# A decoder layer in split float32: the two output tiles of a weight unit take turns term by term

## The reference

```python
x = x + 0.5 * ((silu(h1 @ w1) * (h1 @ w3)) @ w2)        # h1 = rmsnorm(x), hidden width 5632
h = rmsnorm(x)                                          # model width 2048
z = h @ w_in                                            # 8 sections of 1024 columns
oa = block-sparse causal attention(z), or = retention(z), om = cross-attention(z)
gates = sigmoid(h @ w_gate + b_gate)                    # 3 x 2048 columns
merged = g_a * (oa @ w_br_moba) + g_r * (or @ w_br_ret) + g_m * (om @ w_br_mem)
x = x + merged @ w_out
x = x + 0.5 * SwiGLU_2(rmsnorm(x))                      # same shapes as the first line
y = rmsnorm(x)
```

## Time and profile before

| | |
|---|---|
| median of 3 runs | 2692.11 us (2691.68 to 2693.47) |
| span of the profiled execution, first to last instruction | 2688.8 us |
| median less span: what lies around the span | 3.3 us |
| PE busy | 2662.4 us, 99% |
| weight loads (PEld) busy, beside PE | 2590.7 us, 96% |
| DVE busy | 1541.8 us, 57% |
| ACT busy | 1092.0 us, 41% |
| mean rate of DMA | 223 GB/s |

### The profile page before, as it was taken

How to read it: one execution, slowest core, us unless ns; L and a number is a source line. 1 busy time by engine, 2 the same in 40 slices (tenths; PEclk the granted TensorE clock), 3 DMA queues, 4 the chain that set the end, 5 groups by cost and what they waited for, 6 DMA issues and landing times.

```text
span 2688.8 us, 50855 instructions
## 1 busy us (share of the span) xinstructions
PE 2662.4 (99%) x21748; PEld 2590.7 (96%) x21748; DVE 1541.8 (57%) x2442; ACT 1092.0 (41%) x985; POOL 147.5 (5%) x266
## 2 busy tenths in 40 slices
PE   8999999999999999999999999999999999999998
PEld 7899999999999999999998988999999999999998
DVE  4545554555547778876675744365554545555455
ACT  6433333333335433455352444344433333333345
POOL 0000000000000011211211121100000000000000
PEclk9999999999999999999999999999999999999999
DMA  7665555555555799799979899766555555555553
GB/s 267 235 210 186 176 185 182 177 187 177 185 168 175 237 306 299 240 354 392 339 274 334 280 317 320 232 211 198 173 188 175 185 184 177 185 176 186 181 159 115
DMA packets 487449, 600.08 MB, mean 223 GB/s; under 512 B 12608, under 2 KB 447008, under 8 KB 485984
## 3 DMA queue, kind: packets, MB, share of 16 engines
q1 hardware_dynamic: 442512, 456.37, 52.9%
q0 software_dynamic: 35088, 129.74, 13.3%
q10 hardware_dynamic: 9680, 11.54, 1.2%
HBM read 575.16 MB, written 24.53 MB: 223 GB/s over the span
## 4 chain that ended last, share of the span: by engine, by line
PE 96%; DVE 1%; DMA 1%; ACT 1%; issue 1%; DVEq 0%; POOLq 0%; SPq 0%; ACTq 0%
PE PS L554 30%; PE PS L555 29%; PE PS L556 29%; PE PS L1997 1%; PE PS L590 1%; PE PS L592 1%; PE PS L591 1%; DVE splitL L509 1%; DMA raw<-w_gate 1%; ACT splitH L503 1%; PE PS L1760 0%; PE PS L1497 0%; PE PS L1728 0%; PE PS L1242 0%; PE PS L1356 0%
## 5 line engine op out<-in xcount | busy, mean ns | idle before, releaser
L509 DVE TENSOR_TENSOR splitL<-raw,splitH 128x2048 fp32r<-128x2048 f32 (+1 forms) x462 | 1007.5, 2181 | 841.8 <-ACT splitH L503 840.9
L503 ACT ACTIVATE splitH<-raw 128x2048 fp32r<-128x2048 f32 (+1 forms) x462 | 844.4, 1829 | 1493.4 <-PE PS L556 1443.4
L554 PE MATMUL PS<-gH,splitH 128*128 128x264 f32 x3072 | 880.9, 287 | 5.3 <-DVE splitL L509 5.3
L555 PE MATMUL PS<-gL,splitH 128*128 128x264 f32 x3072 | 871.2, 284 | 0.0
L556 PE MATMUL PS<-gH,splitL 128*128 128x264 f32 x3072 | 870.6, 283 | 0.0
L554 PEld LDWEIGHTS PS<-gH,splitH 128*128 128x128 f32 x3072 | 579.3, 189 | 25.0 <-issue 22.9
L555 PEld LDWEIGHTS PS<-gL,splitH 128*128 128x128 f32 x3072 | 579.7, 189 | 0.5 <-issue 0.2
L556 PEld LDWEIGHTS PS<-gH,splitL 128*128 128x128 f32 x3072 | 576.7, 188 | 0.0
L554 PE MATMUL PS<-hH,splitH 128*128 128x264 f32 x1536 | 436.1, 284 | 0.1
L555 PE MATMUL PS<-hL,splitH 128*128 128x264 f32 x1536 | 435.1, 283 | 0.0
L556 PE MATMUL PS<-hH,splitL 128*128 128x264 f32 x1536 | 434.9, 283 | 0.0
(11 more groups left out here) (378 smaller groups left out, 2969.8 us busy)
## 6 DMA issues: line engine op xcount, KB each, us to landing
raw<-ffn_w SPq DMA_DIRECT2D x240, 1024.0 KB, 5.1
raw<-w_in SPq DMA_DIRECT2D x64, 1024.0 KB, 7.2
raw<-w_gate SPq DMA_DIRECT2D x48, 1024.0 KB, 8.0
ring<-cache_k POOLq DMA_DIRECT2D x64, 512.0 KB, 6.0
ring<-cache_v POOLq DMA_DIRECT2D x64, 512.0 KB, 5.8
raw<-ffn_w SPq DMA_DIRECT2D x32, 768.0 KB, 4.8
raw<-w_out SPq DMA_DIRECT2D x16, 1024.0 KB, 5.5
raw<-w_mem_kv SPq DMA_DIRECT2D x15, 1024.0 KB, 6.4
```

The lines of the kernel that those rows point to most:

```text
L503: nc.scalar.activation(splitH[:, s, tiles, :], raw[:, u, 0:nk, :], ACT.Copy).then_inc(hi_ready, 1)
L509: nc.vector.tensor_tensor(splitL[:, s, tiles, :], raw[:, u, 0:nk, :], splitH[:, s, tiles, :].bitcast(F32), ALU.subtract).then_inc(split_re ...
L554: nc.tensor.matmul(out, w_hi, H[:, k, 0:n], start=first, stop=False)
L555: nc.tensor.matmul(out, w_hi, L[:, k, 0:n], start=False, stop=False)
```

## The change

In `pe_unit` the loop over the two output tiles m moves from outside to inside. Before, a unit of 8 tiles issues 24 matmuls into the bank of m = 0 and then 24 into that of m = 1. After, for each weight tile k it issues high-high for m = 0 and m = 1, then high-low for both, then low-high for both, so each matmul goes to another bank than the one before it. The set of matmuls, their operands and the order of additions within each output tile stay. The order in which PE reads weights and activations changes: before, k by k, high weight twice and low weight once, with activation H, L, H; after, the weight alternates between its two column halves and the activations are read as H, H, L, L, H, H. The wait for the second half in the `halves` unit comes after 24 matmuls and no longer after 12.

```diff
-        for m in range(2):
-            out = PS[:, 2 * (u // 2) + m, 0:n]
-            for j, k in enumerate(tiles):
-                if halves and m == 0 and j == UK // 2:
-                    pe.wait_ge(split_ready, 8 * B + 4 * c + u + 1)
-                w_hi = splitH[:, s, kept_at.start + j, m * P:(m + 1) * P]
-                w_lo = splitL[:, s, kept_at.start + j, m * P:(m + 1) * P]
-                first, final = start and j == 0, stop and j == len(tiles) - 1
-                nc.tensor.matmul(out, w_hi, H[:, k, 0:n], start=first, stop=False)
-                nc.tensor.matmul(out, w_hi, L[:, k, 0:n], start=False, stop=False)
-                last = nc.tensor.matmul(out, w_lo, H[:, k, 0:n], start=False, stop=final)
+        outs = [PS[:, 2 * (u // 2) + m, 0:n] for m in range(2)]
+        for j, k in enumerate(tiles):
+            if halves and j == UK // 2:
+                pe.wait_ge(split_ready, 8 * B + 4 * c + u + 1)
+            w_hi = [splitH[:, s, kept_at.start + j, m * P:(m + 1) * P] for m in range(2)]
+            w_lo = [splitL[:, s, kept_at.start + j, m * P:(m + 1) * P] for m in range(2)]
+            first, final = start and j == 0, stop and j == len(tiles) - 1
+            for m in range(2):
+                nc.tensor.matmul(outs[m], w_hi[m], H[:, k, 0:n], start=first, stop=False)
+            for m in range(2):
+                nc.tensor.matmul(outs[m], w_hi[m], L[:, k, 0:n], start=False, stop=False)
+            for m in range(2):
+                last = nc.tensor.matmul(outs[m], w_lo[m], H[:, k, 0:n], start=False, stop=final)
         last.then_inc(unit_used, 1)
```

## The result

The changed kernel takes 2717.27 us (median of 4 runs, 2715.96 to 2720.19) against 2692.79 us for the kernel before on the same chip: a ratio of 1.0087, with a 95% interval from 1.0076 to 1.0099. It is slower by 0.87%, some 24 us. The forecast was 2690 us with a range to 2710.

What follows compares the result with a forecast made beforehand. PE bounds the kernel: 19,968 matmuls times their start-to-start distance of 120.83 ns. Terms 0 + 0 - 2 + 0 = -2 us, on a median of 2692.1 us, gave 2690 us, with a range of 2674 to 2710 us.

Steps and rivals of the forecast that it cites:

- Instructions, repeated loads: 0: In `pe_unit`: same 19,968 matmuls and as many weight loads; losing the repeated weight load costs nothing, 0 us.
- Banks: 0: In `pe_unit`: adding into another bank than the matmul before saves or costs nothing, 0 us; extremes -216 and +100 us.
- The single crossings: Steps where the old kernel changes bank, once a unit: 0.12 us, like steps that stay, read as no bank effect.
- The 10.8 ns over half the slow step: Excess of the 120.83 ns matmul distance over 110 ns, half the 220 ns step seen at 1.2 GHz.
- 216 us ceiling: Most the change could ever give: 19,968 matmuls times the 10.8 ns excess.
- The order of reads: -2 us: `pe_unit` activation reads: fewer moves between tile places, estimated at -4.2 us, taken as -2, allowed from -17 to +17 us.
- one move costs some 1.3 ns: From `h` and `mg` stages: two thirds of a move more per matmul cost 0.85 ns, hence this price per move.
- the 17 us between `mg` and the rest: `mg` stage's 0.85 ns slower matmul over the kernel, the limit for the read order, by symmetry both ways.
- the order costs: Rival: the new read order settles at a dearer pace, as in `mg`; +17 us, 2709 us, chance 25%.
- The prediction's own sign: In the profile after: `h` and `mg` moving by different amounts means addresses matter; both falling alike means the bank.
- Waits: 0: Split weights, loads and bank reading keep their times; the halved `w_out` unit won't wait after 24 matmuls; 0 us.
- The clock: Rival: bank changes at each matmul leave pauses that lower PE's clock; a tenth at half clock +198 us, 2890 us; 3%.

Runs made afterwards that it cites:

- e4_micro: Bare kernel of 30 streams of 192 matmuls, not the layer: 122.2 ns a matmul with activations in the new order, 120.8 to 121.0 in the old.
- e1_banks: Kernel before with its order of reads kept, but consecutive matmuls going to the two banks in turn: 2693.55 us, ratio 1.0001.
- e2_reads: Kernel before with the changed kernel's order of reads, but each half of a unit's matmuls into one bank: 2718.28 us, ratio 1.0092.
- e9_terms: Kernel before with each output tile's matmuls ordered term by term, so the activation tile changes every matmul: 2694.99 us, ratio 1.0001.
- e8_micro_places: Bare streams of 192 matmuls with shifted activations, other low-part distances, other pitches and held tiles: none of 41 shifted or re-pitched streams below 120.8 ns.
- e6_mg_aligned: Kernel before with `mgL` 160 bytes further on, at a multiple of 256 bytes from `mgH`: `mg` stage 92.80 us for 93.45, whole 2692.25 us.
- e5_twopass: Changed kernel's bank change at every matmul, but the unit gone through twice, three matmuls per activation tile each time: 2693.41 us, ratio 0.9996 to kernel before.
- e7_micro_runs: Bare streams of 192 matmuls with other run lengths per activation tile, held tiles and widths: runs of 1 take 120.8 ns, of 2, 4, 6 122.2 to 122.4.

## Why the prediction was wrong, step by step

*What bounds the kernel.* Right. The whole difference is in the distance between matmuls, and one or two nanoseconds of it were enough for the verdict.

*Instructions, repeated loads: 0.* Right. Even a single weight tile for a whole stream left the pace (`e4_micro`, L229).

*Banks: 0.* Right, and shown by `e1_banks` at 1.0001, with 185.60 us in the `h` stretch. The single crossings could not show it that well: they were read to 5 ns either way, where 0.27 ns decide. The 10.8 ns over half the slow step don't hang on the bank, so of the 216 us ceiling nothing was to be had this way.

The Trainium skill, "Perfetto Trace Analysis", section "Matmul Optimizations", asks for all 8 banks to be in use. Between matmul and matmul no run here shows any worth in it: one bank throughout, 24 matmuls in a row per bank, and two banks in turn gave one pace. No stretch of these matmuls used more than four banks.

*The order of reads: -2 us.* **This is the step that failed**, in sign and in size: 0.1 ns a matmul less was forecast, 1.67 ns more was measured in the `h` stretches. With the banks kept out, `e2_reads` shows it to be worth all of the +24 us. It had the right suspect, the place of the moving tiles, but two errors. First, a law was drawn from two points: "one move costs some 1.3 ns". `e9_terms` moves with each matmul and loses nothing. The eleven unaligned distances of the low part in `e8_micro_places` all move with each matmul, and take anything from 121.1 to 122.3 ns. So the number of moves doesn't set the pace. `e6_mg_aligned` takes the 0.85 ns of the `mg` stage away with 160 bytes. Second, the 17 us between `mg` and the rest was taken as a bound on both sides. It was one other value of a quantity that follows no rule found here, not its edge. The `h` stretches went up by 1.67 ns, twice that: 2.56 us in the stretch that the prediction names, where it allowed 1.3. The rival "the order costs", at 25%, named what happened and priced it at 2709 us with the same mis-sized term. The prediction's own sign came true: `h` and `mg` moved by different amounts, 1.67 and 0.4 ns, which it had named as the mark of the addresses. Its last sentence also allowed for a new order with a pace of its own, without a price.

*Waits: 0.* Right: 6.1 us for 5.8, and the halved unit goes through without a stop.

*The clock.* It stayed at full, so that rival is out.

*The sum.* Two slips that decide nothing: the chances outside the range add up to 13% at most (7, 3 and part of 3), not 15. And of the 3.3 us put around the span, some 1.7 lie there (the changed kernel's profiled execution took 2716.26 us with a span of 2714.6); the rest is a difference between executions.

What a reader could have taken from the trace before: the step varied with the tile and recurred with it. The first step on tile 7 is 0.13 us where the mean is 0.12, in a unit of 8 tiles and in one of 6, where it stands at another position. In the trace this step is 129 ns in each of the 64 half units of the stretch. A pace that depends on the sequence of addresses can't be assumed to stay when the sequence changes. The long stretches had been at one value throughout, 120.83 ns, near the cheapest of all that were tried since: at 264 columns only some held tiles and the pitch of 1280 bytes gave less, down to 120.0. From such a place a blind change of order has more room to lose than to gain.

**What stays open.** Why a sequence of starts has the pace it has. The runs show that it depends on the start of the moving tiles, on their order, on the width and on what ran before, and that banks, weights and the number of moves have no part. The paces repeat: three kernels with the new order of reads or turns of three have 188.16 us in the `h` stretch, and `e1_banks` and `e5_twopass` have the 185.60 of the kernel before. But no run shows the mechanism, and none gives a rule to compute the pace from an order. The order of activations is parted from that of weights in the streams alone, not in a whole kernel. The smaller loss in the middle of the kernel, where fp32 matmuls stand between the units, was not taken apart either.

No version beats the kernel before. `e5_twopass` and `e9_terms` equal it. One lead was left: a pitch of 1280 bytes with the old order gave 120.0 to 120.1 ns in `e4_micro` and `e7_micro_runs`, but 121.3 in `e8_micro_places`. At 0.8 ns less it would be worth some 16 us (an estimate, 19,968 x 0.8 ns); no kernel was run with it, and whether the tiles would fit is not shown.

## What to carry to other kernels

When PE is the bound and runs matmul behind matmul, measure the start-to-start distance over a long clean stretch. A nanosecond of it is nearly 1% here, and it can change with nothing but the order or the place of the moving tiles. So an edit that only reorders matmuls is not neutral. A short kernel of bare streams, one order to a line, gave the pace of an order in the `h` stretch within 0.3 ns (122.2 for 122.5, 120.8 for 120.8, 122.3 for 122.3), at some 23 us a stream. It missed the `mg` stage by up to 0.8 ns, with the wrong sign. So try orders and placements in streams first, but believe the kernel alone. And an alternation of PSUM banks is no reason to reorder: it was worth nothing here, to 0.1%.

## What the runs showed of the hardware that was not expected

- At the full clock a matmul of 264 float32r columns takes 120.0 to 126.6 ns by address, order and history; at half the clock it was 220 ns in a steady row, twice 110. The variation was seen only at full speed; the few steps at half the clock were alike.
- With the start of all activation tiles 4 bytes further on, a matmul took 4.5 ns longer, 125.3 for 120.8 ns, in the one stream tried.
- The same held tile ran at 120.0, 120.1 or 121.3 ns within one kernel, by what ran before it; another one at 121.6 ns in one kernel and at 126.6 ns in another, over 192 matmuls each time.
- 260 columns took 118.7 ns and 256 columns 119.9 ns, in one stream each behind different streams. The difference is no larger than what the history of a held tile made above, so that the width alone does this is not shown.

The Trainium skill, "TensorE: Matmul & The Clock Gate", section "Back-to-back issue gap", gives columns divided by 2.4 GHz plus 2.5 ns for a matmul that stands alone, that is 109.2 ns for 256 columns and 112.5 for 264. These matmuls follow each other in streams, and no stream here comes near it: 119.9 and 120.0 ns were the least that the float32r streams show at these widths.
